# One tap of each convolution block moved from TensorE to VectorE, with a GpSimd wait and a changed VectorE order

## The reference

```python
def conformer_conv(h, pw1_w, pw1_b, dw_w, dw_b, ln_g, ln_b, pw2_w, pw2_b):
    a = h @ pw1_w + pw1_b
    u, gate = jnp.split(a, 2, axis=-1)
    u = u * jax.nn.sigmoid(gate)
    y = lax.conv_general_dilated(
        u, dw_w[:, None, :], window_strides=(1,),
        padding=((CONV_WIDTH - 1, 0),),
        dimension_numbers=("NWC", "WIO", "NWC"),
        feature_group_count=D_MODEL) + dw_b
    y = layernorm(y, ln_g, ln_b)
    y = jax.nn.silu(y)
    return y @ pw2_w + pw2_b
```

## Time and profile before

| | before |
|---|---|
| median of three runs | 1132.3 us |
| the profiled execution's own time | 1132.31 us |
| its span | 1130.6 us |
| TensorE busy | 1108.9 us, 98% |
| VectorE busy | 937.8 us, 83% |
| ScalarE busy | 766.7 us, 68% |
| GpSimd busy | 292.8 us, 26% |
| convolution stage, blocks 0 to 7 | about 29 to 151 us of the span |
| taps on VectorE (L2324) in PSUM | x116, mean 750 ns |

### The profile page before, as it was taken

The page is one execution under the profiler, slowest core; times in us unless marked ns, Lnnn a source line. Parts: engine busy times, 40 slices in busy tenths (PEclk is TensorE's granted clock), DMA queues, the critical chain, the costliest instruction groups (busy, mean ns, idle before and its releaser), DMA issues. The chain is left out here.

```text
span 1130.6 us, 18199 instructions
## 1 busy us (share of the span) xinstructions
PE 1108.9 (98%) x6426; PEld 971.2 (86%) x6426; DVE 937.8 (83%) x1363; ACT 766.7 (68%) x1266; POOL 292.8 (26%) x269
## 2 busy tenths in 40 slices
PE   8999999999999999999999999999999999999997
PEld 7788888988998998998977888878887998998986
DVE  5899985779889689688789888884889889688688
ACT  6778877556785583665787777776656783674764
POOL 5688870312120020113421111100312020111024
PEclk9999999999999999999999999999999999999999
DMA  5322133185866577585223333232477777567673
GB/s 171 99 73 74 38 110 92 26 261 127 204 162 139 172 168 184 118 220 112 57 57 86 87 76 77 83 85 75 149 205 158 178 169 183 120 145 191 164 199 100
DMA packets 137268, 146.73 MB, mean 130 GB/s; under 512 B 5949, under 2 KB 108349, under 8 KB 136682
## 3 DMA queue, kind: packets, MB, share of 16 engines
q1 hardware_dynamic: 112300, 109.68, 30.9%
q0 software_dynamic: 24816, 35.92, 19.7%
q10 hardware_dynamic: 78, 0.16, 0.0%
HBM read 137.09 MB, written 6.29 MB: 127 GB/s over the span
## 5 line engine op out<-in xcount | busy, mean ns | idle before, releaser
L1553 ACT ACTIVATE whi<-mraw 128x1024 fp32r<-128x1024 f32 x212 | 221.6, 1056 | 147.9 <-PE psum L1247 95.2
L2238 DVE TENSOR_TENSOR wlo<-mraw,whi 128x1024 fp32r<-128x1024 f32 x212 | 256.6, 1221 | 69.2 <-ACT whi L1553 68.6
L1245 PE MATMUL psum<-whi,aop_hi 128*128 128x512 f32 x448 | 176.0, 393 | 0.9 <-ACT acc L1863 0.9
L1246 PE MATMUL psum<-wlo,aop_hi 128*128 128x512 f32 x448 | 174.5, 390 | 0.0
L1247 PE MATMUL psum<-whi,aop_lo 128*128 128x512 f32 x448 | 174.5, 389 | 0.0
L890 PE MATMUL psum<-hhi,whi 128*128 128x512 f32 x372 | 149.2, 401 | 0.8 <-DVE wlo L2227 0.5
L892 PE MATMUL psum<-hhi,wlo 128*128 128x512 f32 x372 | 145.4, 391 | 0.0
L891 PE MATMUL psum<-hlo,whi 128*128 128x512 f32 x372 | 145.2, 390 | 0.0
L1233 PE MATMUL psum<-hhi,wlo 128*128 128x256 f32 x384 | 108.7, 283 | 0.0
L1232 PE MATMUL psum<-xlo,whi 128*128 128x256 f32 x384 | 108.7, 283 | 0.0
L1231 PE MATMUL psum<-hhi,whi 128*128 128x256 f32 x384 | 108.6, 283 | 0.0
(11 more groups left out here) (333 smaller groups left out, 2833.3 us busy)
## 6 DMA issues: line engine op xcount, KB each, us to landing
mraw<-in_mlp_w_up SPq DMA_DIRECT2D x64, 512.0 KB, 7.0
mraw<-in_mlp_w_down SPq DMA_DIRECT2D x64, 512.0 KB, 5.4
mraw<-in_mlp_w_down POOLq DMA_DIRECT2D x40, 512.0 KB, 6.8
mraw<-in_mlp_w_up POOLq DMA_DIRECT2D x24, 512.0 KB, 6.8
wraw<-in_conv_pw_w SPq DMA_DIRECT2D x20, 512.0 KB, 4.4
wraw<-in_attn_w_in SPq DMA_DIRECT2D x16, 512.0 KB, 4.8
x_copy<-xT SPq DMA_DIRECT2D x2, 2048.0 KB, 7.5
xT<-x_copy SPq DMA_DIRECT2D x2, 2048.0 KB, 11.4
```

Source lines behind the costliest of these rows:

```text
L1245: pe.matmul(o, ah, wh, start=kt == 0 and (not kept or c == 0), stop=False)
L1246: pe.matmul(o, ah, wl, start=False, stop=False)
L1553: a.activation(split_unit(whi, e), raw_unit(l, c, e_), ACT.Copy).then_inc(s["m_hi"], 1)
L2238: d.tensor_tensor(split_unit(wlo, e), raw_unit(l, c, e_), split_unit(whi, e).bitcast(F32), ALU.subtract).then_inc(s["m_ready"], 1)
```

## The change

`PE_TAPS` goes from 7 to 6, and so `DVE_TAPS` from 17 to 18. `y_total` on GpSimd gets a wait on `glu_u`, the semaphore that counts the gated products that VectorE has finished: in round j it waits until that of block j+1 is done. On VectorE `join` moves from behind both evacuations to between them.

```diff
-PE_TAPS = 7
+PE_TAPS = 6
@@
-            def y_total(j, r, last=False):
+            def y_total(j, r, last=False, behind=0):
+                if behind:
+                    pool.wait_ge(s["glu_u"], behind)
                 at_ = y_sums(j + 1) + (0 if last else POOL_SUMS)
                 pool.wait_ge(s["y_done"], j + 1)
@@
                 if j > 0:
-                    y_total(j - 1, 1 - r)
+                    y_total(j - 1, 1 - r, behind=j + 2)
@@
-            def gates(n, r):
+            def gates(n, r, between=None):
@@
                 d.tensor_tensor(tmp[:, 0, :], psum[:, 2 * r + 1, :], rinv[:, :],
                                 ALU.mult).then_inc(s["glu_g"], 1)
+                if between:
+                    between()
                 d.tensor_tensor(tmp[:, 2, :], psum[:, 2 * r, :], rinv[:, :],
                                 ALU.mult).then_inc(s["glu_t"], 1)
@@
-                gates(n, r)
-                if not (isinstance(j, int) and j == 0):
-                    join(j - 1, 1 - r)
+                first = isinstance(j, int) and j == 0
+                gates(n, r, None if first else lambda: join(j - 1, 1 - r))
                 gated(j, r)
```

## The result

| | before | after |
|---|---|---|
| median of six runs each, us | 1131.97 (1131.34 to 1132.61) | 1135.91 (1133.19 to 1137.47) |
| ratio | | 1.0032 [1.0022, 1.0042] |
| profiled execution, its span, us | 1132.31, 1130.6 | 1133.19, 1131.4 |
| TensorE, VectorE, GpSimd busy, us | 1108.9, 937.8, 292.8 | 1106.0, 938.7, 289.5 |

The change makes the kernel 3.9 us slower, 0.3%. I had forecast 1132.8, and 1134.3 as the upper end.

What follows compares the result with a forecast made beforehand. VectorE, in a 15.89 us ring with GpSimd, was taken to set the stage's end by when it reaches `join(6)`. +0.66 + 0.68 - 0.24 - 0.62 = +0.5 us turned 1132.31 into 1132.8, range 1131.2 to 1134.3.

Steps and rivals of the forecast that it cites:

- blocks 0 and 1: VectorE's first two blocks of the convolution stage: forecast to take +0.66 and +0.68 us more.
- Blocks 2 to 5: VectorE's four loop rounds: forecast 63.42 us instead of 63.66, so -0.24.
- The idle time ahead of `conv`: TensorE was to wait for `u_lo` ahead of each `conv`, about 0.7 us a block.
- TensorE's last tap matmul: End of TensorE's taps: forecast at about 149.6 us, 150.22 before, and still ahead of L2422.
- three evacuations and `join` ahead of the gated product: VectorE, loop: work before the gated product, starting it 2.05 and 2.24 us behind the first evacuation; 1.92 in block 6.
- A rule of the Trainium skill: VectorE and GpSimd sharing SBUF ports, loser blocked fully: 1.25 us saved a block, sum -0.5; set aside for 1.05.
- block 6, "0.66 for its gated product": VectorE, block 6: 17.36 us instead of 17.98, so -0.62, with 0.66 counted for block 7's gated product.
- the long gated product: VectorE's gated product, held by GpSimd's block sum L689: forecast to fall by 1.05 us to 0.75.
- the 0.26 us wait: VectorE's wait for TensorE at 130.53 in block 6: 0.26 us, counted as going within that block's -0.62.
- the five products: GpSimd, loop: products ending 14.4 us behind a gated product's end, clear of the next one, which begins after 14.9.
- the clock, 0.12 and "up to 1.7 us": Rival, after the taps: the 1.2 GHz stretch slides into the dense row at 159.07, costing up to 1.7 us, 1134.5; chance 0.12.

Runs made afterwards that it cites:

- `fix7`: The changed kernel with one of GpSimd's two product sums ahead of block 7's `u_lo` moved behind it; 1134.56 us, ratio 1.0021.
- `all_three`: The changed kernel with `join` back behind both evacuations, one GpSimd product sum moved behind block 7's `u_lo`, six unread matmuls after the last `conv`; 1132.23 us.
- `fixwarm`: The changed kernel with one GpSimd product sum moved behind block 7's `u_lo` and six unread matmuls after the last `conv`; 1134.05 us, ratio 1.0015.
- `warm6`: The changed kernel with six unread 128x128 matmuls added on TensorE after the last `conv`; 1134.63 us, ratio 1.0018.
- `again`: The changed kernel, unaltered, timed and profiled again; 1135.29 us, ratio 1.0024.
- `taps_only`: The kernel before with only `PE_TAPS` lowered from 7 to 6, without the new wait or the move of `join`; 1136.35 us, ratio 1.0032.

## Why the prediction was wrong

**What held.** Counted from block 0's first evacuation, blocks 0 and 1 added 0.67 and 0.68 (0.66 and 0.68 forecast). Blocks 2 to 5 took 0.27 off (0.24). The gated product started 2.22 and 2.04 behind the first evacuation in the two halves of the loop (2.24 and 2.05), and 1.92 in block 6, as forecast; `u_lo` came 2.71 behind its end (2.75). The idle time ahead of `conv` was 0.16 to 0.87 us, mostly 0.45, where I had said about 0.7; but from start to start a block loses 15.83 - 15.09 = 0.74, as forecast. TensorE's last tap matmul stood at 149.40 (149.6 forecast), and that is luck: counted from block 0's first evacuation it came 0.15 sooner and not 0.6. (The prediction speaks of three evacuations and `join` ahead of the gated product; there are two, and its 1.92 counts two.) A rule of the Trainium skill was rightly set aside: SBUF — State Buffer, section "SBUF: two separate sides", has the loser blocked fully, which would put block 7's gated product 0.75 behind GpSimd's end; the trace has 0.55 again.

**The step that failed in the sum: block 6, "0.66 for its gated product".** Block 7's gated product took 1.30. I took its 0.74 from the trace of before, but there VectorE had come to it 0.22 us behind the end of GpSimd's product sum (129.45 + 2.72 = 132.17, start at 132.39). From block 6's first evacuation VectorE now needs 8.68 us to it and no longer 9.95, since it lost the long gated product and the 0.26 us wait, both of which I had subtracted; the sum ends only 0.30 sooner (9.43 for 9.73). I had checked `u_lo` and the five products against the block sum, but not the products of the written-out block, which are added in another order, against the gated product. Block 6 gave 0.06 and not 0.62, and the stage lost 1.02 and not 0.5. `fix7` takes 0.53 of it back. The same 0.55 us reach TensorE through `u_lo` of block 7, and are what its last tap matmul lacks to the forecast. L2418 stood at +0.35 in after's profile only because that execution started 0.67 early.

**The step that failed in the chances: the clock, 0.12 and "up to 1.7 us".** Cause and place were right, the victim wrong. I let the low stretch slide backward into the dense row at 159. It slid forward, onto the one-column matmuls of the statistics, which I had called thin and so held to be cheap. They are thin in TensorE's work, but VectorE's L2473 waits for them, and at 1.2 GHz they cost 2.2 us (2.45 over the whole statistics), where I had allowed 1.7 at most. Nor was the stretch free where it lay before: there it costs 0.6, before and after alike. I had the piece for this: TensorE ends 0.6 earlier and VectorE 0.5 later, so a gap of 0.31 us ahead of the statistics grows past one. (It became 1.49, from 0.15 and 1.02: the right size from two wrong parts.) And I gave it one chance in eight, while about two of three executions were low.

**The size.** Means over all runs put the change at about +3.1 us (1135.7 of 15 runs against 1132.5 or so). The stage holds 1.0 of it. The clock holds about 2/3 x 2.2 = 1.5, an estimate from the share of low runs and from what they take more than the others (1136.4 against 1134.2). The remaining 0.6 or so is open. It is of the size by which start and rest differ between any two profiles; that kernels with six taps have both somewhat longer (rest 972.7 in the mean of eight profiles, 972.3 of four with seven) isn't told apart from chance.

**What the change is, then.** The tap costs VectorE 0.66 a block; the removed collision would pay for it; but `join` ahead of the second evacuation takes 1.24 back, and block 7's new collision 0.53. With both repaired and fillers added, `all_three` equals the kernel before. No version here beats it.

## What to carry to other kernels

A saving of TensorE time that only becomes idle time can cost: look at what follows the gap, and if it is a chain of small matmuls that another engine waits for, price it at both levels of the clock, because that chain is where the lower level hurts. When one wait is removed from a round, recheck each later meeting of the two engines, in written-out first and last rounds above all: a shift of under a microsecond makes a clear pair collide. Don't move an independent instruction away if that leaves a dependent one right behind its parent: `join` had filled a wait of 0.12 us in written-out code and of 0.24 in the loop. And count positions from a fixed point of the stage: a trace that starts 0.67 us early made two wrong terms look right.

## What the runs showed of the hardware

- Six 128x128 matmuls into an idle time of 1.5 us made low runs rarer in each of three pairs: 2 of 11 against 10 of 15, 3 of 11 (`fixwarm`) against 10 of 11, 5 of 11 (`all_three`) against 9 of 11. One of the three profiles has no low stretch behind the taps, two have one of 3.4 us.
- What a stretch at 1.2 GHz costs depends on what it meets: 3.4 us cost 0.6 over four 128x128 matmuls that VectorE waits for (after against `warm6`), 0.5 in a dense row (`all_three`), 10.2 us cost 3.0 (`again` against `warm6`), and 1.8 to 5.0 us at the end of the span met no matmul.
- The same code, run again, had its clock fall at 154.7 for 3.4 us or at 153.0 for 10.2 us. One profile of a kernel need not show its median execution: after's was 2.7 us under the median of its six runs.
- A VectorE product with two SBUF inputs that meets a GpSimd sum ended 0.55 us behind it, whether it was issued 0.04 us behind the sum's start, lasting 1.80, or, at block 7, some 0.6 behind the start of the second of two sums, lasting 1.30. In `taps_only` it met the sum later still and lasted 0.95 to 1.16.
- The first evacuation came 29.0 to 30.1 us from the span's start, and an accumulating transfer needed 7.1 to 8.1 us to its use, in different profiles: each about 1 us, where the change's own effect is 3 to 4.
